# Experts' stage of a hybrid encoder block: where VectorE makes the low parts of a new expert's up weights

## What is computed

```python
xs = xt[tok_s]
a = jax.nn.silu(lax.ragged_dot(xs, w_gate, sizes)) * lax.ragged_dot(xs, w_up, sizes)
ys = lax.ragged_dot(a, w_down, sizes) * weight.reshape(-1)[order][:, None].astype(h.dtype)
out = jnp.zeros_like(xt).at[tok_s].add(ys)
...
h = _layernorm(alpha * h + ffn, ln2_g[l], ln2_b[l])
```

## Time and profile before

| | |
|---|---|
| median of 3 runs | 4194.5 us (4185.06 to 4198.86) |
| profiled execution | 4199.52 us |
| its span, first to last instruction | 4197.5 us |
| mean granted TensorE clock | 0.988 of full speed |
| PE busy / PEld busy | 4076.5 us (97%) / 3395.4 us (81%) |
| DVE / ACT / POOL busy | 2073.1 / 1439.2 / 744.8 us |

### The profile page before, as it was taken

The page is one execution under the profiler, slowest core; times in us unless marked ns, Lnnn a source line. Parts: engine busy times, 40 slices in busy tenths (PEclk is TensorE's granted clock), DMA queues, the critical chain, the costliest instruction groups (busy, mean ns, idle before and its releaser), DMA issues. The chain is left out here.

```text
span 4197.5 us, 60770 instructions
## 1 busy us (share of the span) xinstructions
PE 4076.5 (97%) x20066; PEld 3395.4 (81%) x20067; DVE 2073.1 (49%) x3202; ACT 1439.2 (34%) x2543; POOL 744.8 (18%) x1020
## 2 busy tenths in 40 slices
PE   8999999999999999999999998699999999999997
PEld 7888888888888888888888887587888888788886
DVE  3554443443443443443443444577656567665664
ACT  2422311311311311311311311366556456555553
POOL 2000010000000001001001001234333333433333
PEclk9999999999999999999999998799999999999998
DMA  8787456456456455456455555676756566665562
GB/s 251 241 306 244 145 202 204 156 198 196 159 199 195 166 200 187 169 197 187 175 197 184 175 197 186 217 254 222 252 187 205 188 219 229 228 211 190 195 218 81
DMA packets 278468, 840.53 MB, mean 200 GB/s; under 512 B 47952, under 2 KB 99408, under 8 KB 226688
## 3 DMA queue, kind: packets, MB, share of 16 engines
q1 hardware_dynamic: 228400, 716.61, 50.2%
q0 software_dynamic: 49936, 121.90, 8.7%
HBM read 717.60 MB, written 178.45 MB: 213 GB/s over the span
## 5 line engine op out<-in xcount | busy, mean ns | idle before, releaser
L1110 PE MATMUL bank<-hT_hi,w_slot 128*128 128x512 f32 x2176 | 862.3, 396 | 8.3 <-DVE w_slot L898 7.2
L1112 PE MATMUL bank<-hT_hi,w_slot 128*128 128x512 f32 x2176 | 848.9, 390 | 0.0
L1111 PE MATMUL bank<-hT_lo,w_slot 128*128 128x512 f32 x2176 | 848.1, 390 | 0.0
L1742 PE MATMUL e_bank<-e_w_hi,e_xT_hi 128*128 128x512 f32 x1312 | 522.7, 398 | 18.2 <-DVE e_xT_lo L1668 15.8
L1744 PE MATMUL e_bank<-e_w_hi,e_xT_lo 128*128 128x512 f32 x1312 | 514.7, 392 | 0.0
L1743 PE MATMUL e_bank<-e_w_lo,e_xT_hi 128*128 128x512 f32 x1312 | 513.9, 392 | 0.0
L1673 DVE TENSOR_TENSOR e_w_lo<-e_raw,e_w_hi 128x1024 fp32r<-128x1024 f32 x384 | 444.1, 1220 | 116.7 <-ACT e_w_hi L1624 116.7
L1110 PEld LDWEIGHTS bank<-hT_hi,w_slot 128*128 128x128 f32 x2176 | 409.0, 188 | 105.8 <-issue 24.6
L1112 PEld LDWEIGHTS bank<-hT_hi,w_slot 128*128 128x128 f32 x2176 | 408.9, 188 | 87.4
L1111 PEld LDWEIGHTS bank<-hT_lo,w_slot 128*128 128x128 f32 x2176 | 409.5, 188 | 81.2
L1624 ACT ACTIVATE e_w_hi<-e_raw 128x1024 fp32r<-128x1024 f32 x376 | 366.2, 1054 | 2.0 <-issue 2.0
(11 more groups left out here) (330 smaller groups left out, 6712.7 us busy)
## 6 DMA issues: line engine op xcount, KB each, us to landing
w_slot<-split_weights SPq DMA_DIRECT2D x353, 1024.0 KB, 4.8
e_raw<-in_w_exp_gate_dram SPq DMA_DIRECT2D x128, 512.0 KB, 6.0
e_raw<-in_w_exp_up_dram SPq DMA_DIRECT2D x128, 512.0 KB, 6.1
e_raw<-in_w_exp_down_dram SPq DMA_DIRECT2D x128, 512.0 KB, 5.4
split_weights<-w_slot SPq DMA_DIRECT2D x50, 1024.0 KB, 5.7
h_rows<-h_rows SPq DMA_DIRECT2D x64, 512.0 KB, 7.7
x_rows<-in_x_dram SPq DMA_DIRECT2D x32, 512.0 KB, 5.5
raw<-in_w_in_dram SPq DMA_DIRECT2D x30, 512.0 KB, 7.2
```

What stands on the lines that cost most here:

```text
L1110: pe.matmul(out, hi, x_hi, start=first, stop=False)
L1111: pe.matmul(out, hi, x_lo, start=False, stop=False)
L1112: return pe.matmul(out, lo, x_hi, start=False, stop=last)
L1742: pe.matmul(out_p, hi, x_hi, start=first, stop=False)
```

## The change

On DVE, the four subtractions that make the low parts of an expert's up weights move. Before, they are done for expert e + 1 in the last tile of expert e, behind `normalise` and ahead of `e_aT_lo`. After, they are done for expert e at the very head of its first tile, behind the old tile's `e_aT_lo` and `add_base` and behind the head of the expert loop. For expert 0 they stay ahead of the loops: the list that did all eight chunks is cut to the gate's four, and the up chunks follow in tile 0. Nothing else is changed.

```diff
--- before.py
+++ after.py
@@ -1704,13 +1704,16 @@
                 v.sem_inc(y_taken, 2)
                 v.wait_ge(down_lo, DC)
                 v.sem_inc(down_set, 1)
-                for c in range(2 * GC):
+                for c in range(GC):
                     split_lo(0, c)
                 evacuate(0)
                 v.wait_ge(consts_in, 32)
                 with v.Fori(0, E) as e:
                     lo, hi, swap = tiles_of(v, e)
                     with v.Fori(lo, hi) as g:
+                        with v.If(g == lo):
+                            for c in range(GC, 2 * GC):
+                                split_lo(e, c)
                         with v.If(g == swap):
                             for c in range(GC):
                                 split_lo(e + 1, c)
@@ -1719,9 +1722,6 @@
                         v.tensor_tensor(prod[:, :], up_p[:, :], act[:, :], ALU.mult).then_inc(prod_ready, 1)
                         evacuate(g * 2 + 2)
                         normalise(g - 2)
-                        with v.If(g == swap):
-                            for c in range(GC, 2 * GC):
-                                split_lo(e + 1, c)
                         v.wait_ge(a_hi, g + 1)
                         v.tensor_tensor(aT_lo[:, :, :], aT_p[:, :].rearrange("p (k c) -> p k c", k=KF),
                                         aT_hi[:, :, :].bitcast(FP32), ALU.subtract).then_inc(a_ready, 1)
```

## The result

The changed kernel takes 4258.84 us (median of 3 runs, 4255.56 to 4261.12) against 4194.5: 1.0159 times the time before, interval 1.0136 to 1.0182, or +64 us. The forecast was 4214, its range ended at 4248. It was right that the change costs time, and wrong by 45 us about how much.

A forecast was written before the change was run, and what follows sets the result against it. PE was taken as full (busy over 97%), with POOL's loop nearly as long. 18 + 7 + 21 - 25 - 4 + 3 = +20 us on the profiled 4199.5; the runs' median is 5 lower: 4214, range 4190 to 4248.

The forecast's parts named there:

- The floor: At 30 joins, PE waits 0.6 us for the first up low part behind the loop head: +18 (0 to 30).
- The one-tile expert: At expert 6's join, VectorE must also make four down low parts before the up ones: +7 us (5 to 8).
- What comes back: Experts' stage: today's losses shrink as POOL is less late, -25 us; earlier add_base shortens POOL's waits, -4 us.
- Late base rows: At joins, add_base's wait for e_base reaches PE; only the largest of neighbouring late joins counts: +21 us (10 to 53).
- The moved loads: SyncE's next up loads start some 3 us later, meeting the scatter instead of the e_rows gather: costed at nothing.
- The clock: PE after new waits of 3 us and more: three or four run slow, 1.4 to 2.7 us each: +3.
- The fourth rival: At each join the short PE wait halves the clock: +79 us with other terms, 4274; 4 in 100.
- The third: Base rows paid in full, POOL's transfers colliding anew with weight loads: +63 us, 4258; 9 in 100.
- The first and second: Rivals: loop head hidden under aT_lo and add_base, about 4167, 7 in 100; penalty and returns balance, 4196, 26 in 100.
- C: Experiments' theory: up loads released later meet POOL's scatter in an expert's first tile, and POOL has no slack.

The follow-up runs named there:

- e3: Changed kernel with the low parts at the new expert's head, outside the inner loop, and the old tile's add_base behind them: 4223.64 us.
- f1: Changed kernel with up loads of experts behind the first cut to 8 of 128 partitions: 4200.77 us.
- g1: Changed kernel with store_part ahead of store_rows on POOL's queue: 4194.45 us.
- e4: Kernel before, low parts in place, with the next up loads held until VectorE enters the next expert: 4267.92 us.
- f2: Kernel before with up loads of experts behind the first cut to 8 of 128 partitions: 4175.56 us.
- f3: Changed kernel with each up load issued only when the one ahead has landed: 4245.24 us.
- e1: Kernel before with the up low parts moved down between aT_lo and add_base in the old expert's last tile: 4205.76 us.

## Why the prediction was wrong

**The floor: right.** "I take 0.6 a join", +18. Measured 0.75, so 23.3. PE's named wait is 0.45 at such a join (median); the rest is the restart. e3, with nothing but the head in front, has 0.2.

**The one-tile expert: right.** +7. Measured 8.6 above the floor, of which 2.7 are slow clock, so 5.9 for the mechanism itself. It stands in f1 and g1 too (join excess 9.4 and 10.0 us), which do away with the long joins.

**What comes back: right.** -25 and -4. All that PE loses outside the joins' gate and up products fell by 34.1 - 8.8 = 25.3.

**Late base rows: the step that failed.** "But a PE that waits lets POOL catch up, so in a run of neighbouring late joins only the largest counts", +21. Measured: 61.9 above the floor at 13 joins, of which 15.7 are slow clock (below): 46.2. The mechanism was named, and the upper bound of 53 held it; the choice of the low value failed. POOL does catch up, 13 late joins for 21; but with full loads the lead that a stop gives it is used up by the next join but one. f1 shows the discount as it was forecast, once the loads are small; g1 shows it with full loads and a shorter chain.

**The moved loads: the same error from its other side.** "I see no sign for the balance", cost nothing. The 3 us by which the loads move was right at the median (3.2; 4.5 at the mean), the scatter in place of the gather of `e_rows` was the right pair, and the balance had a sign. In the first tiles the scatter went from 3.98 to 6.50 us, 2.5 x 30 = 76 us more; the gathers of `e_rows` gave back 30 and the other scatters 14. Summed from issue to landing over the three transfers that POOL waits for in each tile, the time in flight rose from 1316.5 to 1344.1 us, by 28. In e4 it rose by 72 (to 1388.1), close to that run's cost of 76, and POOL waits for PE there as seldom as before (3 tiles). e4 is no price for the loads in the change: its burst has a lead of 2.0 us over the scatter where that of the change has none, and it issues its four loads in 2.16 us for 3.78. Of the change's 64, f1 and f2 put 39 down to the bytes of these loads; the late rows with their clock came out 61.9 - 21 - 3 = 38 over the forecast. I read both as one cost, not two (that they are the same microseconds is argued, not shown): the loads make `e_base` late, and the new order hands the lateness to PE.

**The clock: too small.** +3 for "the three or four largest". Ten joins ran on at half clock and lost 18.4 us by it (for products 0.3 to 0.6 us apart, what that is over 0.23, less the 0.2 that every restart shows): nine of the 13 (15.7) and the one behind the one-tile expert (2.7). In these the products stood 4.2 to 6.7 us apart at the stop; at the 21 that kept their clock 0.8 to 3.7 us. A gap of 2.8 us in f1 and one of 2.4 in f3 halved it too, so the length of one stop doesn't decide alone. The fourth rival, every join, is wrong. The Trainium skill ("TensorE: Matmul & The Clock Gate", section "Why this matters for your kernels") warns that long idle gaps between bursts of matmuls drop the array to half rate. The ten stops agree with it. It speaks of long gaps only, and 20 of the other 21, below 2.5 us, kept the clock; but so did the one of 3.7, and the two of 2.8 and 2.4 did not.

**The rivals.** The third, base rows in full because POOL's transfers collide anew with the weight loads, is what happened, and its 4258 is the measured time. It stood at 9 in 100 because I asked how long `e_base` takes and not how much slack POOL has; the 5 waits of `e_x_at` for PE in 82 tiles were there to be read in the kernel before. That the sum fits to a microsecond is partly luck: it has 53 for the late rows (46.2) and nothing for the clock (18.4), and gives back 15 (25.3, and the 5.6 that the first tiles lost before). The first and second, in which POOL recovers or nothing moves, are out.

Not settled: the 14 us of e1, in which the scatter of first tiles takes 4.45 us for 3.98 and the burst moves by the length of `aT_lo` alone. It fits C; nothing tells it apart from the small waits for `e_xT_lo` (14.3 us for 10.3).

## What to carry to other kernels

Before work is moved on an engine, count how often the neighbouring queue waits for the busiest engine: if it hardly ever does (here 5 tiles of 82), it has no slack to discount the delays of its transfers with; here counting all of them came closer (53 us) than counting the largest of each run (21), for a measured 46.2. A subtraction that frees a load buffer is also the load's clock: moving it moves 2 MB of transfers per expert, and moving these alone cost 76 us here (e4). And a wait placed ahead of urgent work turns lateness that cost the up products nothing (`e_base` late at 21 of 31 joins before) into stops of the engine that bounds the kernel.

## What I had not expected of the hardware

- A scatter of 512 KB by row index, waited for 2.28 us when four loads of 512 KB were issued 7 us ahead of it, was waited for 6.64 us when they were issued 1.9 us ahead.
- After a stop with 4.2 us or more between two products, at all ten such joins, 7 to 13 products ran on at half clock, 0.43 us apart for 0.23. The clock stayed up at gaps of 0.8 to 3.7 us, though gaps of 2.8 us in f1 and 2.4 us in f3 brought it down.
- The head of a hardware loop with three register loads kept VectorE's queue for 2.0 us at the mean beside other work, and up to 3.3 us.
